# Head sums of two triangular levels, woven into the k steps of a neighbouring projection unit

## What is computed

```
z = a @ w_in                      # q, k, v, gates, pooling input: 9 column blocks
diff = bi[:, :, :, None, :] - bi[:, :, None, :, :]
decay = jnp.exp(jnp.where(mask, diff, -jnp.inf))
attn = jnp.einsum('bhid,bhjd,bhijd->bhij', qi, ki, decay)
o = jnp.einsum('bhij,bhjv->bhiv', attn, vi) + ...
```

## Time and profile before

| | |
|---|---|
| median of 3 runs | 1163.2 us (1162.75 to 1165.55) |
| the profiled execution, its own time | 1161.71 us |
| its span, first to last instruction | 1159.7 us |
| PE busy, matmul records | 1137.3 us, 98% of the span |
| PE weight loads | 944.1 us, 81% |
| DVE, ACT, POOL | 644.0 (56%), 405.8 (35%), 566.4 us (49%) |
| mean granted clock of PE | 0.994 |

### The profile page before, as it was taken

The page is one execution under the profiler, slowest core; times in us unless marked ns, Lnnn a source line. Parts: engine busy times, 40 slices in busy tenths (PEclk is TensorE's granted clock), DMA queues, the critical chain, the costliest instruction groups (busy, mean ns, idle before and its releaser), DMA issues.

```text
span 1159.7 us, 15145 instructions
## 1 busy us (share of the span) xinstructions
PE 1137.3 (98%) x5650; PEld 944.1 (81%) x5650; DVE 644.0 (56%) x754; ACT 405.8 (35%) x639; POOL 566.4 (49%) x366
## 2 busy tenths in 40 slices
PE   9999999999999989999999999999999999989997
PEld 7788999787888678888888888888888888868886
DVE  7565576548548954444444445454535454874444
ACT  8401112154324442323233333333233233464334
POOL 0011275214236676656665656565656565693202
PEclk9999999999999999999999999999999999999999
DMA  6211111113100111111111111111111110501003
GB/s 248 90 37 37 38 38 37 37 73 146 55 10 10 55 55 55 54 54 54 55 54 54 54 54 54 54 54 54 54 54 54 54 44 11 196 4 46 10 1 145
DMA packets 25189, 67.96 MB, mean 59 GB/s; under 512 B 2560, under 2 KB 5696, under 8 KB 23232
## 3 DMA queue, kind: packets, MB, share of 16 engines
q1 hardware_dynamic: 25152, 67.44, 16.5%
HBM read 63.24 MB, written 4.19 MB: 58 GB/s over the span
## 4 chain that ended last, share of the span: by engine, by line
PE 37%; POOL 30%; issue 24%; DVE 5%; ACT 1%; DMA 1%; POOLq 1%; SPq 0%; DVEq 0%; ACTq 0%
POOL r_lo L568 17%; PE pb L1561 10%; PE pb L1563 10%; PE pb L1562 10%; POOL raw_b L586 4%; POOL raw_a L584 3%; POOL s_sum L579 2%; POOL raw_a L582 2%; PE pb L1688 2%; DVE t_raw L1367 1%; POOL sums L653 1%; PE pb L1672 1%; PE pb L1649 1%; PE pb L1634 1%; PE pb L1669 1%
## 5 line engine op out<-in xcount | busy, mean ns | idle before, releaser
L1433 DVE TENSOR_TENSOR h<-h,pb 128x512 f32<-128x512 f32 x176 | 116.7, 681 | 51.1 <-PE pb L1563 49.9
L502 POOL TENSOR_TENSOR w_lo<-w_raw,w_hi 128x2048 fp32r<-128x2048 f32 x10 | 49.4, 4942 | 186.8 <-ACT w_hi L675 140.9
L1784 PE MATMUL pb<-t_hi,r_hi 128*128 128x512 f32 x352 | 137.6, 391 | 2.8 <-issue 1.6
L568 POOL TENSOR_TENSOR r_lo<-raw_b,r_hi 128x512 fp32r<-128x512 f32 x63 | 91.2, 1448 | 94.2 <-ACT r_hi L811 94.2
L1786 PE MATMUL pb<-t_hi,r_lo 128*128 128x512 f32 x352 | 137.0, 389 | 0.0
L1785 PE MATMUL pb<-t_lo,r_hi 128*128 128x512 f32 x352 | 136.9, 389 | 0.0
L568 POOL TENSOR_TENSOR r_lo<-raw_a,r_hi 128x512 fp32r<-128x512 f32 x63 | 84.2, 1336 | 91.2 <-ACT r_hi L811 91.2
L1561 PE MATMUL pb<-gu_hi,r_hi 128*128 128x512 f32 x320 | 124.5, 389 | 0.0
L1562 PE MATMUL pb<-gu_lo,r_hi 128*128 128x512 f32 x320 | 124.5, 389 | 0.0
L1563 PE MATMUL pb<-gu_hi,r_lo 128*128 128x512 f32 x320 | 124.5, 389 | 0.0
L811 ACT CAST r_hi<-raw_b 128x512 fp32r<-128x512 f32 x63 | 39.2, 622 | 203.8 <-POOL raw_b L586 144.9
(11 more groups left out here) (238 smaller groups left out, 2643.6 us busy)
## 6 DMA issues: line engine op xcount, KB each, us to landing
raw_d<-in_w_ffn_down_dram SPq DMA_DIRECT2D x22, 512.0 KB, 3.5
w_raw<-in_w_in_dram SPq DMA_DIRECT2D x7, 1024.0 KB, 4.9
raw_a<-in_w_ffn_gate_dram SPq DMA_DIRECT2D x11, 512.0 KB, 3.4
raw_b<-in_w_ffn_gate_dram SPq DMA_DIRECT2D x11, 512.0 KB, 4.6
raw_a<-in_w_ffn_up_dram SPq DMA_DIRECT2D x10, 512.0 KB, 3.5
raw_b<-in_w_ffn_up_dram SPq DMA_DIRECT2D x10, 512.0 KB, 4.4
h<-in_x_t_dram SPq DMA_DIRECT2D x16, 256.0 KB, 6.1
w_raw<-in_w_out_dram SPq DMA_DIRECT2D x4, 1024.0 KB, 4.7
```

Source lines behind the costliest of these rows:

```text
L502: nc.gpsimd.tensor_tensor(w_lo[s][:, 0:size], w_raw[s][:, 0:size], w_hi[s][:, 0:size].bitcast(F32), ALU.subtract).then_inc(w_lo_ready[s], 1)
L568: nc.gpsimd.tensor_tensor(r_lo[q % RING][:].rearrange("p (k n) -> p k n", k=kts), src, r_hi[q % RING][:].bitcast(F32).rearrange("p (k n) - ...
L1433: V.tensor_tensor(h[:, m, both(c)], h[:, m, both(c)], aux.bank(F_DOWN + n)[:], ALU.add).then_inc(aux.drained, 1)
L1784: M(bank[:], wh[:, k, :], x_h[:, k, :], start=start and k == 0, stop=False, skip_group_check=True)
```

## The change

Diag and near no longer stand as blocks of 16 matmuls behind units (3, 1) and (6, 2). Their matmuls are issued within these units. For diag, four of them stand ahead of each of the k steps 4 to 7 of unit (3, 1); the wait for `qk_ready` and the claim of the bank stand ahead of k step 4. For near, one stands ahead of each of the 16 k steps of unit (6, 2); the wait for `near_ready` and the claim stand ahead of the first step. The matmuls, their operands and their banks are the same, and the other engines' lists are not touched.

```diff
-            def v_unit(n, s, j):
+            def v_unit(n, s, j, ready=None):
...
                     for k in range(KT):
+                        if ready is not None:
+                            ready(t % 2 * KT + k)
                         i = split3(bank, a_hi[:, k, rows], a_lo[:, k, rows], wh[:, k, :], wl[:, k, :], k == 0, k == KT - 1)
...
-                elif kind == "diag":
-                    pe.wait_ge(qk_ready, 1)
-                elif kind == "near":
-                    pe.wait_ge(near_ready, 1)
...
-                elif kind in ("diag", "near"):
-                    sc = scaled[:, 1 if kind == "diag" else NEAR % 2, :].rearrange("p (a t c) -> p t a c", a=KP, c=C)
-                    for j in range(NCH * KP):
-                        i = M(bank[:, 2 * j:2 * j + 2], sc[:, j // KP, j % KP, :], head_ones[:], start=True, stop=True)
...
+            def head_sums(f, part, j):
+                i = M(aux.bank(f)[:, 2 * j:2 * j + 2], scaled[:, part, :].rearrange("p (a t c) -> p t a c", a=KP, c=C)[:, j // KP, j % KP, :],
+                      head_ones[:], start=True, stop=True)
+                if j == NCH * KP - 1:
+                    i.then_inc(aux.filled, 1)
+
+            def diag_sums(k):
+                f = FILL["diag", 0]
+                if k == 4:
+                    pe.wait_ge(qk_ready, 1)
+                    aux.claim(f)
+                if k >= 4:
+                    for j in range(4 * (k - 4), 4 * (k - 3)):
+                        head_sums(f, 1, j)
+
+            def near_sums(step):
+                f = FILL["near", 0]
+                if step == 0:
+                    pe.wait_ge(near_ready, 1)
+                    aux.claim(f)
+                head_sums(f, NEAR % 2, step)
...
+                    elif kind in ("diag", "near"):
+                        continue
...
-                        v_unit(u, s, j)
+                        v_unit(u, s, j, ready=near_sums if (b, j) == (6, 2) else None)
...
-                             ready=query_ready if (b, j) == (2, 0) else None)
+                             ready={(2, 0): query_ready, (3, 1): diag_sums}.get((b, j)))
```

## The result

The changed kernel takes 1170.06 us in the median of 20 runs (1161.57 to 1173.72), the one before 1163.26 us (1161.79 to 1165.55). The medians are 6.8 us apart. The recorded ratio, which is not that of the two medians, is 1.0046 with an interval of 1.0033 to 1.0059: slower, where I had forecast no change. The 20 runs are two groups: 7 between 1161.57 and 1164.39 us, with a mean granted clock of 0.996 or 0.997, and 13 between 1169.12 and 1173.72 us, at 0.985 to 0.990. I call them early and late runs. The profiled execution (1163.87 us, span 1161.8) is an early one, so its profile shows the change at its best. A profile of a late run, of the kernel with only near woven, follows with the experiments.

What follows compares the result with a forecast made beforehand. PE, busy 98% of the span, was taken as the bound unless its next start is held. 1161.7 us, +0.1 at (4, 0), -0.1 at (7, 0), median 1.5 above: 1163.2 us, no change; range 1160.8 to 1165.6.

Steps and rivals of the forecast that it cites:

- A woven sum costs as much as one in a block: Units (3, 1) and (6, 2): weaving hides nothing; diag 3.62 us against 3.59, near taken at 3.6 us.
- the upper of my two bounds: Near's woven sums in (6, 2): cost between nothing and 3.6 us; 3.6 was taken.
- The reading by which loads pulled ahead hide the sums: Rival at diag and near: woven sums are free, (4, 0) moves by -3.5 us, time 1159.6 us; chance 0.06.
- Diag gains nothing because w_lo of block 4 follows it: Start of (4, 0): w_lo ends 0.85 us later, PE idles about 1.7 us, (4, 0) moves by +0.1 us.
- the wait of 1.25 us: Ahead of (6, 2): PE's bank claim waits for DVE's drain of level 5's first fill, a new 1.25 us stall.
- (7, 0) held by w_lo of block 7: Start of (7, 0): no earlier than 189.87 whatever near's sums cost, a change of -0.1 us.
- k_scale in time: DVE behind near: k_scale takes 4.43 us and ends at 194.25, 1.25 us ahead of the kt fills at 195.50.
- Does the clock stay up?: Woven (3, 1) and (6, 2): both falls of the clock vanish, PE's own stream 3.3 us shorter.
- the price of a fall: PE at half clock for about 3.3 us: a fall costs PE about 1.65 us.
- the clock falls in the woven stretches: Rival in (3, 1) and (6, 2) or (6, 3): falls cost up to 1.65 us each, time 1166.5 us; chance 0.06.

Runs made afterwards that it cites:

- e2: Changed kernel with only diag woven, near a block again behind (6, 2): 1163.98 us, 1.0005 against the kernel before.
- e12: Changed kernel with near woven from step 4 without PE's wait, and ACT's copies of blocks 4 to 7 one exponential earlier: 1159.09 us, 0.9964 against the kernel before.
- e9: Changed kernel with near's sums and waits from step 4 of (6, 2) to step 3 of (6, 3), diag woven: 1163.97 us, 1.0005 against the kernel before.
- e4: Kernel before with only near's waits moved ahead of (6, 2), its sums still a block: 1164.87 us, 1.0015.
- e5: Changed kernel with diag a block, near woven from step 4 of (6, 2) to step 3 of (6, 3): 1163.32 us, 0.9992 against the kernel before.
- e1: The changed kernel again, no edit: ratio 1.0056 against the kernel before; two of nine runs early, seven late.
- e3: Changed kernel with only near woven, diag a block again: 1170.84 us, 1.0059 against the kernel before.
- e11: Changed kernel with diag a block, near in four groups of four sums in (6, 2), wait kept: 1164.84 us, 1.0028 against the kernel before.
- e6: Changed kernel with diag a block, one near sum every second k step of (6, 2) and (6, 3), wait kept: 1164.72 us, 1.0009 against the kernel before.
- e10: Kernel before with only ACT's copies of blocks 4 to 7 one exponential earlier: 1161.77 us, 0.9989.
- e8: Changed kernel with near woven from step 4 without PE's wait, and ACT's copies of blocks 4 to 7 earlier: 1160.41 us, 0.9977 against the kernel before.

## Why the prediction was wrong

**A woven sum costs as much as one in a block: right.** 0.92 us for eight records against 0.91, and 3.6 us for near's sixteen, the upper of my two bounds. The reading by which loads pulled ahead hide the sums was wrong here for both forms.

**Diag gains nothing because w_lo of block 4 follows it: right.** (4, 0) moved by 0.04 us (forecast 0.1), with a wait of 1.54 us (1.7). e2, diag alone, is 1.0005. e12's early (4, 0) shows that the hold was POOL's.

**Near: the wait of 1.25 us: right in size**, 1.25 us, released by line 1251. **(7, 0) held by w_lo of block 7: a tie** in the early run, where PE and `w_lo` come within 0.01 us of each other; e9, in which PE comes earlier and waits 1.20 us, shows that `w_lo` is the bound I took it for. **k_scale in time: right**; it ends at 193.93, `kt` starts at 197.44, and it took 2.38 us instead of 4.43 because only its first 0.23 us met POOL's `w_lo`. I had left it at 4.43.

**"Does the clock stay up?" - "I take it that both falls vanish": this step failed.** Diag's and near's falls did vanish in the profile after, but the wait that replaced the gain can bring a new one (97.6 to 100.9 in the profile after). For near it failed in two ways. I compared a woven step with level 0's fills, but not the wait and the woven steps together: e4 has the wait without weaving, e5 and e9 weaving without the wait, and only both together gave late runs in number (20 of 29 in the changed kernel and e1, 6 of 6 in e3, 5 of 11 in e11, against none of 22 in e5 and e9). I had written the wait of 1.25 us down as a plain delay that `w_lo` hides.

**And the price of a fall was wrong by a factor of more than four: its length, not its rate.** I had this case as a rival, "the clock falls in the woven stretches", at 0.06 and up to 1.65 us a fall, because the two falls in the trace of before ended after 3.3 us. They ended while PE had only large matmuls to do. In (6, 2) the sums fill the unit, and the clock stays down: e3 shows 17 us at 0.50, 7.7 us of PE's time. e6, with the sums half as dense, is back after 3.2 us. Nothing hides this: in the early run PE and `w_lo` of block 7 come to (7, 0) together, so whatever PE loses ahead of it counts in full. With this price the rival's time would have been about 1163.2 + 7, which is where the late runs lie, and the range would have had to reach there.

The rival with the Trainium skill (TensorE: Matmul & The Clock Gate, section A second HAM failure mode: psum-queue depth-cycling), frequent micro-idles between groups, was the nearest to what happened, though what the trace shows is not a clock going up and down but one that stays down. I had set it aside because level 0's fills kept 1.00. They begin at full clock; e3 shows what such a mixture does once the clock is down.

**Still open:** what decides in a given run whether a fall comes. The same kernel had 9 early and 20 late runs, and the early profile and e3's late one have the same first sum at 176.68. The short falls come and go too: behind diag's block (there in the kernel before, not in e10), and behind the wait at (4, 0) (there in the profile after, not in e2). And e5 and e9 move the sums by four steps besides taking the wait away; a version with the same steps and no wait would need another bank, and was not tried. The changed kernel was not run beside either of them.

## What to carry to other kernels

Here small matmuls woven into a unit cost as much as in a block. What weaving can give is the clock, so ask what holds the next start before counting the gain. A wait moved ahead of a stretch full of small matmuls may not be a delay of its own length: when the clock fell there, the stretch was paid at half speed to its end. Put the claim of a bank where it has long been drained; e9, e8 and e12 did so and had no late run. And take many runs: one early profile hid 7 us here.

## What the runs showed of the hardware

The granted clock can stay at 1.2 GHz for 17 us while PE is never idle (e3, 178.9 to 195.8). For the first 13 us of it PE was in a unit in which two of five weight loads belong to two-column matmuls, then in (6, 3) with large ones alone. The same unit, behind the same wait, runs through at 2.4 GHz in other executions (0.58 us a step instead of 1.06). The clock fell behind idle times of 1.24 to 1.54 us next to fills of small matmuls (e3 and e6 at (6, 2), the changed kernel at 97.6), and stayed up behind 1.25 and 1.56 us in others (the changed kernel at (6, 2), e2 at (4, 0)). Ahead of (6, 0) it fell behind 0.83 us in e5 and e11 and stayed up behind 0.97 us before. The two falls of the kernel before had a block of sums ahead of them.

The end of DVE's k_scale followed POOL's `w_lo`, not its own start. In four profiles it starts while `w_lo` of block 7 runs, at four different times (187.54 before, 189.99 in e4, 190.70 in e9, 191.55 after), takes 4.43, 2.66, 3.32 and 2.38 us, and ends 2.15 us behind `w_lo` each time.
